# A hybrid decoder layer in float32: prompt attention with the values of two heads in alternate matmuls

## The reference, cut to what matters

```python
def step(S, inp):                       # sampled and prompt recurrence, per head
    r_t, w_t, k_t, v_t, kk_t, a_t = inp
    sa = jnp.einsum('bhij,bhj->bhi', S, -kk_t)
    S = (S * w_t[:, :, None, :] + sa[..., :, None] * (kk_t * a_t)[..., None, :]
         + v_t[..., :, None] * k_t[..., None, :])
    return S, jnp.einsum('bhij,bhj->bhi', S, r_t)
...
s_own = jnp.einsum('tcgd,scd->tcgs', qg, k_own) * scale      # prompt attention
s_own = jnp.where(causal[:, None, None, :], s_own, NEG_INF)
p = jax.nn.softmax(jnp.concatenate([s_sel, s_own], axis=-1), axis=-1)
...
mix = jnp.concatenate([att, rw], axis=-1) @ w_out
```

## Time and profile before

| | |
|---|---|
| median of 3 runs | 3145.16 us (3141.46 to 3146.03) |
| the profiled execution | 3146.96 us |
| its span | 3145.3 us |
| mean granted clock | 0.984 |
| TensorE busy | 3004.0 us (96%), weight loads 2424.1 |
| DVE, ACT, POOL busy | 2019.7, 827.7, 295.8 us |
| DMA | 322.59 MB, mean 103 GB/s |

### The profile page before, as it was taken

The page is one execution under the profiler, slowest core; times in us unless marked ns, Lnnn a source line. Parts: engine busy times, 40 slices in busy tenths (PEclk is TensorE's granted clock), DMA queues, the critical chain, the costliest instruction groups (busy, mean ns, idle before and its releaser), DMA issues.

```text
span 3145.3 us, 53452 instructions
## 1 busy us (share of the span) xinstructions
PE 3004.0 (96%) x20730; PEld 2424.1 (77%) x20730; DVE 2019.7 (64%) x3809; ACT 827.7 (26%) x1945; POOL 295.8 (9%) x516
## 2 busy tenths in 40 slices
PE   8999999999999888899899999999999999999997
PEld 6888778887765566677688888888888877888776
DVE  4444566656898433316966766766766678877887
ACT  1000144431315533301322222222222233222234
POOL 0000011100000444405000000000000000000002
PEclk9999999999999999999899999999999999999999
DMA  6233000003210687750233233233233234432321
GB/s 171 81 81 87 24 10 11 10 20 105 80 48 4 198 251 239 248 185 17 87 100 125 93 104 125 83 113 125 75 121 124 72 114 156 134 131 95 101 86 71
DMA packets 338063, 322.59 MB, mean 103 GB/s; under 512 B 20601, under 2 KB 323686, under 8 KB 336408
## 3 DMA queue, kind: packets, MB, share of 16 engines
q1 hardware_dynamic: 323284, 278.66, 28.3%
q0 software_dynamic: 14528, 40.52, 4.1%
HBM read 296.37 MB, written 22.74 MB: 101 GB/s over the span
## 4 chain that ended last, share of the span: by engine, by line
PE 85%; DVE 7%; issue 3%; ACT 2%; DMA 1%; POOLq 1%; POOL 0%; SPq 0%; DVEq 0%; ACTq 0%
PE ps L1287 45%; PE ps L810 11%; PE ps L874 7%; PE ps L755 6%; PE ps L1120 4%; PE ps L1259 4%; PE ps L1080 1%; PE ps L1108 1%; PE ps L1177 1%; PE ps L1216 1%; DMA W<-in_cache_k_dram 1%; POOLq L447 1%; PE ps L1159 1%; DVE BIG L2268 1%; PE ps L1099 0%
## 5 line engine op out<-in xcount | busy, mean ns | idle before, releaser
L1287 PE MATMUL ps<-BIG,UA 128*128 128x272 f32 x2288 | 539.0, 392 | 0.8 <-ACT UV L1852 0.4
L1287 PEld LDWEIGHTS ps<-BIG,UA 128*128 128x128 f32 x2288 | 434.6, 190 | 91.1 <-issue 1.6
L1287 PE MATMUL ps<-XT,UA 128*128 128x272 f32 x1400 | 331.6, 392 | 0.0
L1287 PEld LDWEIGHTS ps<-XT,UA 128*128 128x128 f32 x1400 | 266.0, 190 | 54.8
L1287 PE MATMUL ps<-BIG,DA 128*128 128x272 f32 x1200 | 294.3, 394 | 9.6 <-ACT UV L1953 3.2
L1287 PEld LDWEIGHTS ps<-BIG,DA 128*128 128x128 f32 x1200 | 227.0, 190 | 60.1 <-issue 12.1
L755 PE MATMUL ps<-XT,W 128*128 128x272 f32 (+1 forms) x832 | 194.5, 395 | 1.7 <-ACT XT L1564 0.9
L755 PEld LDWEIGHTS ps<-XT,W 128*128 128x128 f32 (+1 forms) x832 | 153.9, 185 | 43.8 <-issue 5.8
L874 PE MATMUL ps<-BIG 64*64 64x64 f32 (+1 forms) x3072 | 146.5, 234 | 21.3 <-DVE BIG L2268 12.7
L874 PEld LDWEIGHTS ps<-BIG 64*64 64x64 f32 x3072 | 128.4, 138 | 35.1 <-DVE BIG L2268 19.8
L1287 PE MATMUL ps<-BIG 128*128 128x272 f32 x432 | 108.8, 393 | 1.8 <-issue 1.7
(11 more groups left out here) (633 smaller groups left out, 5451.9 us busy)
## 6 DMA issues: line engine op xcount, KB each, us to landing
BIG<-in_w_up_dram SPq DMA_DIRECT2D x176, 512.0 KB, 5.8
W<-in_w_in_dram SPq DMA_DIRECT2D x38, 1024.0 KB, 5.7
BIG<-in_w_down_dram SPq DMA_DIRECT2D x96, 384.0 KB, 3.7
W<-in_cache_k_dram SPq DMA_DIRECT2D x128, 128.0 KB, 3.4
W<-in_cache_k_dram POOLq DMA_DIRECT2D x128, 128.0 KB, 3.7
W<-in_cache_v_dram SPq DMA_DIRECT2D x128, 128.0 KB, 3.5
W<-in_cache_v_dram POOLq DMA_DIRECT2D x128, 128.0 KB, 3.6
h_keep<-H SPq DMA_DIRECT2D x22, 544.0 KB, 2.7
```

What stands on the lines that cost most here:

```text
L1287: last = nc.tensor.matmul(ps[:, bank, 0:HALF], weights[:, k], x[:, k], start=start and k == 0, stop=k == kc - 1, skip_group_check=not start)
```

## The change

- The value matmuls of an even head are held back until the odd head that follows, and the two heads' matmuls then alternate in the loop over the four blocks, one writing partitions 0 to 63 and the other 64 to 127.
- Scores are made two heads ahead (`PR` has three buffers). The ten transposes go into three banks with 512, 384 and 384 columns, so ACT makes three copies for four. ACT also copies the output out of bank 7, in place of DVE.
- The turn of keys and values stands inside the tile's matmuls (before contraction step 10 of 16). `KDUP` is laid out by ACT. The last rotation stands behind the scores of head 0.
- SP issues the eight loads of sampled vectors before the last state of the chain is stored; POOL loads half of the states before the end of the chain. `WKV`, from which the state is stored, moves to the area of slots 1 and 2, and slot 2's first load waits for the stores.
- The passes of the sampled recurrence are dealt anew: 9, 7, 5, 6, 6, 5, 5, 5, 5, 6, 6 and 2 in the tiles, and behind heads 1, 3, 5, 7 (one each) and 9 (two).
- Of the output projection's tiles, 4, 8 and 12 stand in the key phases of groups 1 to 3 behind chunk 4, in banks 6 and 7; the others follow in order, and tile 14 stands in the last value phase.

```diff
-        WKV = carve("w3", CHUNK)
+        WKV = carve("w12", CHUNK)
-        PR = [BIG[:, F0 + 2048 + 1280 * j:F0 + 3328 + 1280 * j] for j in range(2)]
+        PR = [BIG[:, o:o + 1280] for o in (F0 + 2048, F0 + 3328, F0 + 7168)]
-        GAP_TILES = [(0,), (4,), (8,), (12,)]
-        VALUE_TILES = [{1: 1, 3: 2, 5: 3}, {1: 5, 3: 6, 5: 7}, {1: 9, 3: 10, 5: 11}, {3: 13}]
+        KEY_TILES = [(), (4,), (8,), (12,)]
+        GAP_TILES = [(0,), (5,), (9,), (13,)]
+        VALUE_TILES = [{1: 1, 3: 2, 5: 3}, {2: 6, 5: 7}, {2: 10, 5: 11}, {3: 14}]
+        half_bank = lambda i: 6 if i in (4, 8, 12) else 2 * (i % 2)
...
                     load_in(ATT_ORDER[0], 0, 7)
+                    sp.wait_ge(S["sv_out"], 16 * PAIRS + 16)
+                    sp.wait_ge(S["solve_dve"], after("solve_dve", "p3", 2 * PAIRS, 1))
+                    for b in range(DEC_BATCH):
+                        sp.dma_start(SV_ROWS[b * 16:b * 16 + 16], dec_vecs[...]).then_inc(S["sv_in"], 16)
                 sp.wait_ge(S["wkv_ev"], p + 1)
...
+            for t in range(1, ATT_TILES):
+                if t == 2:
+                    sp.wait_ge(stored, 18 * 16 + 16 * PAIRS)
                 load_in(ATT_ORDER[t], t % 3, 7 + t // 3)
...
             for t in range(ATT_TILES):
-                dense(t % 3, 7 + t // 3, RW_TILES + t, t % 2)
+                def turn_keys():
+                    pe.wait_ge(acc_free, RW_TILES + t + 2)
+                    pe.wait_ge(S["rope_ev"], max(2, t - 3))
+                    keys_values(t - 4, 4)
+                dense(t % 3, 7 + t // 3, RW_TILES + t, t % 2, half_way=turn_keys if 4 <= t < 8 else None)
...
+            pe.wait_ge(acc_free, RW_TILES + ATT_TILES + 2)
             head_scores(0)
+            rotate(len(ROPE_TILES) - 1)
             for n in range(16):
-                if n < 15:
-                    head_scores(n + 1)
+                if n == 0:
+                    head_scores(1)
+                if n < 14:
+                    head_scores(n + 2)
...
                 for a in range(4):
-                    pe.wait_ge(S["pt_ev"], 4 * n + a + 4)
+                    pe.wait_ge(S["pt_ev"], 3 * n + min(a, 2) + 1)
                     toff = sum(4 - x for x in range(a)) * P
-                    last = nc.tensor.matmul(ps[rows, 7, a * P:512], KVT[:, a, 256 + v * HD:256 + (v + 1) * HD], PT[b][:, toff:toff + (4 - a) * P],
-                                            start=a == 0, stop=a == 3, skip_group_check=True)
+                    for h in range(2):
+                        last = nc.tensor.matmul(ps[64 * h:64 * h + 64, 7, a * P:512], KVT[:, a, 256 + v * HD:256 + (v + 1) * HD],
+                                                PT[h][:, toff:toff + (4 - a) * P], start=a == 0, stop=a == 3, skip_group_check=True)
...
+                    if c == 4:
+                        for i in KEY_TILES[bp]:
+                            pe.wait_ge(S["dec_ev"], bp + 1)
+                            half_tile(i)
...
-            half_tile(14)
             turn_output(3)
             half_tile(15)
...
+            def output(q):
+                act.wait_ge(S["ao_mm"], q + 1)
+                nc.scalar.activation(ZT[:, q, 0:SEQ], ps[:, 7, :], ACT.Copy).then_inc(S["ao_ev"], 1)
...
+                    if a < 3:
+                        act.wait_ge(S["pt_mm"], 3 * n + a + 1)
+                        toff, w = ((0, 4 * P), (4 * P, 3 * P), (7 * P, 3 * P))[a]
+                        nc.scalar.activation(PT[n % 2][:, toff:toff + w], ps[:, 4 + a, 0:w], ACT.Copy).then_inc(S["pt_ev"], 1)
...
+            RECUR = [(7, 2), (4, 3), (2, 3), (2, 4), (2, 4), (2, 3), (2, 3), (2, 3), (2, 3), (2, 4), (2, 4), (2, 0)]
...
+            HEAD_PASSES = {1: 1, 3: 1, 5: 1, 7: 1, 9: 2}
```

More of the change, by code:

```diff
@@ L753, in dense @@
                 for k in range(KT):
+                    if half_way and k == 10:
+                        half_way()
                     for h in range(2):
@@ L1697, in keys_values, with double_keys @@
                 nc.scalar.activation(KVT[0:n, a], ps[0:n, bank, :], ACT.Copy).then_inc(S["kvt_ev"], 1)
+            def double_keys():
+                act.wait_ge(S["gn_chain"], 4 * PAIRS + 2)
+                act.wait_ge(S["gn_ev"], PAIRS)
+                act.wait_ge(S["swap_mm"], 1)
+                for kv in range(4):
+                    m, own = divmod(kv, 2)
+                    for e in range(2):
+                        rows = slice(e * 64, e * 64 + 64)
+                        src = ZT[rows, 8 + m, 0:SEQ] if e == own else ps[rows, 6 + m, :]
+                        l = nc.scalar.activation(KDUP[rows, kv], src, ACT.Copy)
+                l.then_inc(S["qk_laid"], 1)
             for t in range(ATT_TILES):
-                evac(t % 3, 7 + t // 3, ATT_ORDER[t], t % 2)
                 if 4 <= t < 8:
                     keys_values(t - 4, 4)
+                evac(t % 3, 7 + t // 3, ATT_ORDER[t], t % 2)
                 group_norm(t)
+                if t == PAIRS + 1:
+                    double_keys()
             keys_values(4, 6)
-            act.sem_inc(S["pt_ev"], 3)
             def block_exps(n, k):
@@ L2284, in recurrence @@
                 for half in range(2):
-                    dve.wait_ge(S["state_in"], 32)
+                    dve.wait_ge(S["state_in"], 16 * half + 16)
+                    if half == 0:
+                        dve.wait_ge(S["pair_pool"], PAIRS + 1)
+                        first_step[0] = linked[0] + 1
                     SDh = SD[half]
@@ L2344, in _ @@
                     nc.vector.tensor_copy(MASK[:, 3 * P:4 * P], const("causal")).then_inc(S["att_chain"], 1)
[L2345 to L2357 removed]
+                recur(RECUR[t][1])
             def sample_queries(pair):
@@ L2476, in _ @@
                         sample_norm(c // 2 - 1)
+                    if c == 5:
+                        for i in KEY_TILES[bp]:
+                            half_tile(i)
                 if bp == 0:
@@ L3279, in _ @@
                     operands(p + 1)
+            pool.wait_ge(S["lora_mm"], 3 * PAIRS + 1)
+            pool.wait_ge(S["exp_ev"], 4 * PAIRS)
+            pool.wait_ge(S["lprev_ready"], PAIRS)
+            pool.dma_start(SD[0], st_v[:, 0:32]).then_inc(S["state_in"], 16)
             pool.wait_ge(S["wkv_ev"], PAIRS)
             pool.wait_ge(S["ld_ready"], PAIRS + 1)
-            for half in range(2):
-                pool.dma_start(SD[half], st_v[:, 32 * half:32 * half + 32]).then_inc(S["state_in"], 16)
+            pool.wait_ge(S["dve_chain"], first_step[0])
+            pool.dma_start(SD[1], st_v[:, 32:64]).then_inc(S["state_in"], 16)
             pool.wait_ge(S["rec_half"], 1)
```

124 lines of the change are left out of this document (54 added, 70 removed).

## The result

The changed kernel takes 3105.38 us, the median of four runs (3102.85 to 3112.21), where the kernel before took 3144.3 us on the same chip (four runs, 3141.46 to 3146.03): a ratio of 0.988, with a 95% interval from 0.9862 to 0.9898. The profiled execution took 3104.03 us, 42.9 less than that of before; its span is 3101.9 us at a mean granted clock of 0.986.

What follows compares the result with a forecast made beforehand. The prediction took TensorE's own work as the bound. Sampled attention starting 31.0 us earlier plus 5 us gained in it made 36 us off the profiled 3146.96, 3111.0, or 3109 on the median's scale; forecast 3110 us, range 3098 to 3126.

Steps and rivals of the forecast that it cites:

- What bounds the kernel, the loop: Prompt attention: TensorE's own work, 96.6 us of the stage's 99, is the bound; waits are some 2 us.
- Values in alternate matmuls: Prompt attention loop: value matmuls of two heads overlap, 2.5 us a pair, a gain of 18.1 us.
- The skill's rule on weight loads: Rival, prompt attention values: no overlap and 128 bare loads of 0.136 us, 17.4 us more; 3145 us, chance 0.02.
- Transposes: Prompt attention loop: ten transposes a head stay at 1.60 us, as before.
- ScalarE's copies: Prompt attention loop: values wait for ScalarE's copies, 0.2 us a pair, and 1.0 us for the last pair.
- Scores two heads ahead: Prompt attention loop: same work with one more head of slack; DVE's 8.7 to 11.0 us a pair hidden against 10.4.
- Turns: Input projection, four tiles that turn keys and values: four waits of 0.77 us gone, 3.1 us; the turns remain.
- Sampled loads and deal: Input projection: DVE's first pass starts near 718, 7 passes fit there, 67 for 60 in the stage; cost 0.
- Handover: Last turn to first transposes: 922.9 to 934.5, with idles of 1.4 and 1.3 us; bounds 932 and 942.
- forecast's own case: Whole kernel: 31 us before sampled attention plus 5 in it, forecast 3110 us (3103 to 3117), chance 0.58.
- the second rival: Handover: the clock falls in its idles, about 8 us of matmuls cost double; 3118 us, chance 0.18.
- Sampled attention: Sampled attention: fewer key page waits and slow time moved to tile 15, 5 us less, 316 us long; bounds 0 and 16.

## Why the prediction was right, and where it was wrong

The total came out (36 forecast; 38.9 in the medians, 36.5 in the profiled stages that the change touches), and partly for the wrong reasons. Part of it is luck: from the last turn to the sampled attention the forecast had 11.6 + 79.6 = 91.2 us and the profile has 15.0 + 76.5 = 91.5, so a handover 3.4 us too short in the forecast was met by a loop 3.1 us too long.

*What bounds the kernel, the loop.* Wrong. "TensorE's own work is the bound, waits are some 2 us" rested on 96.6 us of durations in a stage of 99. These were spacings of starts, and a spacing holds the waits within a run of matmuls too. In full pace a head is 2.35 of scores, 1.24 of transposes and 2.03 of values: 5.62 us for the 6.33 of the earlier trace rows, and 11.4 us of the stage were waits (16 x 0.71). Close below the old pace of 12.67 us a pair stood a floor of 12.0, the round through DVE and ScalarE with one head of lead: the alternation and the packed copies, put into the kernel before, came down to it and lost the rest to the clock; a head less of lead lost 26.1 us. The waits view of before, with 19.4 and 6.0 us of weight loads waiting for ScalarE, was the row to read, and the forecast did not read it.

*Values in alternate matmuls.* The mechanism is right: 2.55 us a pair, forecast 2.5. The gain is mis-sized, 12.1 and not 18.1, since the 38.1 us that it was taken from had 5.6 us of waits in it (16 x 0.35), and the pair takes 0.05 us more than forecast. The skill's rule on weight loads (the Trainium skill, TensorE: Matmul & The Clock Gate, Part 3, What overlaps and what doesn't), by which the loads of the pair would stand bare since both heads use all rows, does not hold here: the pair's 2.55 us against 4.06 in series show it, since sixteen loads of 0.136 us, 2.2 us, don't fit into them beside the matmuls. The chance of 0.02 given to it was small enough.

*Transposes.* "1.60 us" was wrong too: 1.24, for the third copy no longer has to empty a bank for the fourth. That is 16 x 0.36 = 5.8 us less than the forecast laid in. From the first transposes to the sampled attention it had 79.6 us and the profile has 76.5: against the 5.8 us less of transposes stand 0.4 more of values, some 1.6 more of waits for ScalarE's copies (next) and 1.3 of the first pair at the lower clock (8.85 us from 931.69 to 940.54 for 7.5 at full pace); 0.6 of the difference stays unexplained.

*ScalarE's copies.* Forecast 0.2 us a pair and 1.0 at the end, measured 0.43 a pair and 0.46 + 0.69 at the end.

*Scores two heads ahead.* "Same work, one more head of slack", costed at nothing, was the step that let all others count. The estimate that DVE has room with the new deal was right: 47.9 of 60 us, and 56.1 with the old one.

*Turns.* Forecast 3.1, measured 3.8 in their stage (205.9 against 202.1); of the net effect nothing could be told, since the handover took part of it back.

*Sampled loads and deal.* The first pass starts right behind the chain, as forecast. Late loads cost 3.6 us in the handover. The forecast had said of late loads that the handover would stay as it was, and it does nearly: 18.6 us for 20.0.

*Handover.* The forecast's own case had two idles (1.4 and 1.3 us) and a clock that stays up. The first came as 1.77 us and brought the clock down, so the second rival is what happened: first transposes 15.0 us behind the last turn, and not 11.6. Its price was put at 8 us; against the forecast's own case it was 3.4 in the handover and 1.3 in the first pair of the loop. At the lower clock the scores take so long that the wait for the maxima goes under them. The "against" of that rival, a wait of 3.10 us in a key phase followed by transposes at full pace, did not carry over: a wait of 1.77 us here did what 3.10 us there did not.

*Sampled attention.* Forecast 5 us less and 316 long; measured 4.7 and 316.5, and 5 to 8 us by the kernel with the tiles back, nearly all of it waits for key pages, as it had said. The last tile at the lower clock came out about as long as before (10.17 for 9.60), moved to tile 15 as the forecast had it.

## What to carry to other kernels

Where an engine looks busy for 96 of 99 us, take each of its runs at the pace that it has elsewhere in the trace and read the waits on the weight loads' side too, before calling it the bound: a ring of three engines with one item of lead hides its latency in short stalls within runs. Work taken off such an engine brings little until the lead is longer (here 0.7 us a pair at the upper clock, and nothing once the clock fell in the new waits), and with it everything; so a change of several parts can't be priced part by part against the old schedule. And a short wait costs more than its length when the clock falls behind it: here one pass of the recurrence, put behind another head, took 1.2 us of waiting and 4 us of slow matmuls out of the handover.

## What was not expected of the hardware

- A short wait brought the clock down. In the changed kernel the granted clock is 1.00 from 912 to 919 us; TensorE then idles 1.77 us, and from 920.8 it is 0.50, until 934.5. Two of the other kernels have the same wait (1.79 us, with the tiles back and with the values in series) and the same fall, within some 2 us behind it, and in the latter it lasts until 945. Where only 0.59 us of waiting were left (the pass moved) the clock fell 2.5 us behind that wait for 3.4 us, and where none was left (the swap sooner) it stayed at 1.00. With one head ahead, waits of 1.4 to 2.0 us in front of the transposes left it at 0.89 on average (940 to 1020 us). But the wait of 3.10 us in a key phase did nothing of the kind; what tells them apart is open.
- Two groups of 64 columns of the array with all 128 rows overlap to 2.55 us where they take 4.06 in series, 1.6 times (2.39 us, 1.7 times, in the old order); four groups of 32 reach 3.5 times in the earlier trace rows. They do it with weight loads of 0.136 us before every matmul.
